# Turning queries and mixed outputs with TensorE's transposition instead of a full product with the mirrored identity

## What is computed

```python
for i in range(DEPTH):                                   # DEPTH = 2
    hn = rmsnorm(h, norm_mix[i])
    if i % 2 == 0:
        h = h + swa_sink_mixer(hn, mem_n, ...)           # 12 heads over a window of 128, 4 memory heads
        h = h + swiglu(rmsnorm(h, norm_ffn[i]), ...)
    else:
        h = h + dilated_mixer(hn, mem_n, ...)            # 3 groups of 4 dilated heads, 4 memory heads
        h = h + moe_swiglu(rmsnorm(h, norm_ffn[i]), ...) # top 2 of 8 experts
return rmsnorm(h, final_norm)

def swa_sink_mixer(h, mem_n, table, w_in, sinks, w_mem_kv, w_out):
    q, k, v, qm = split(einsum('bsd,de->bse', h, w_in))
    o, _ = banded_attention(q, k, v, bias, SWA_WINDOW - 1, sinks)
    om = memory_attention(qm, mem_n, w_mem_kv)
    return einsum('bse,ed->bsd', concatenate([o, om], axis=-1), w_out)
```

## Time and profile before

| what | value |
|---|---|
| median of three runs | 1370.65 us |
| lowest and highest run | 1369.57 and 1371.57 us |
| span of the profiled execution, from its first to its last instruction | 1369.3 us |
| PE busy | 1346.9 us, 98% |
| DVE busy | 1130.6 us, 83% |
| ACT busy | 968.0 us, 71% |
| read from HBM | 431.60 MB, 316 GB/s over the span |

### The profile page before, as it was taken

How to read it: one execution, slowest core, us unless ns; L and a number is a source line. 1 busy time by engine, 2 the same in 40 slices (tenths; PEclk the granted TensorE clock), 3 DMA queues, 4 the chain that set the end, 5 groups by cost and what they waited for, 6 DMA issues and landing times.

```text
span 1369.3 us, 18974 instructions
## 1 busy us (share of the span) xinstructions
PE 1346.9 (98%) x6545; PEld 1077.7 (79%) x6545; DVE 1130.6 (83%) x998; ACT 968.0 (71%) x904; POOL 13.7 (1%) x26
## 2 busy tenths in 40 slices
PE   9999999999999999999999999999999999999997
PEld 7888888888887787777777777778777778777775
DVE  6566554444554779999999999999999999999997
ACT  6553643333363468888888888888888887888886
POOL 1100000000000000000000000000000000000000
PEclk9999999999999999999999999999999999999999
DMA  9812655555451049999999999999999999999993
GB/s 375 312 58 107 228 184 184 184 186 189 147 215 62 18 158 400 423 422 422 422 419 357 421 422 422 421 421 367 395 421 422 422 422 393 386 421 422 422 422 162
DMA packets 61402, 433.28 MB, mean 316 GB/s; under 512 B 7066, under 2 KB 7241, under 8 KB 10032
## 3 DMA queue, kind: packets, MB, share of 16 engines
q1 hardware_dynamic: 59312, 426.80, 77.5%
q0 software_dynamic: 1888, 5.78, 1.3%
q10 hardware_dynamic: 160, 0.14, 0.0%
HBM read 431.60 MB, written 1.09 MB: 316 GB/s over the span
## 4 chain that ended last, share of the span: by engine, by line
PE 91%; DVE 4%; ACT 2%; issue 2%; DMA 1%; ACTq 0%; DVEq 0%; SPq 0%
PE ps L1470 20%; PE ps L1472 19%; PE ps L1471 19%; PE ps L1870 6%; PE ps L1869 6%; PE ps L1885 3%; PE ps L1884 3%; DVE wlo L918 2%; PE ps L1915 2%; PE ps L1803 1%; PE ps L1599 1%; PE ps L1572 1%; PE ps L1477 1%; PE ps L1911 1%; PE ps L1923 1%
## 5 line engine op out<-in xcount | busy, mean ns | idle before, releaser
L918 DVE TENSOR_TENSOR wlo<-raw,whi 128x2048 fp32r<-128x2048 f32 (+1 forms) x403 | 908.8, 2282 | 102.0 <-PE ps L1472 62.9
L548 ACT ACTIVATE whi<-raw 128x2048 fp32r<-128x2048 f32 (+1 forms) x403 | 766.2, 1916 | 125.4 <-PE ps L1472 41.9
L1470 PE MATMUL ps<-whi,xhi 128*128 128x512 f32 (+1 forms) x880 | 346.6, 394 | 5.1 <-DVE wlo L918 2.6
L1471 PE MATMUL ps<-wlo,xhi 128*128 128x512 f32 (+1 forms) x880 | 342.0, 389 | 0.0
L1472 PE MATMUL ps<-whi,xlo 128*128 128x512 f32 (+1 forms) x880 | 342.0, 389 | 0.0
L1470 PEld LDWEIGHTS ps<-whi,xhi 128*128 128x128 f32 x880 | 165.3, 188 | 44.7 <-DVE wlo L918 7.5
L1472 PEld LDWEIGHTS ps<-whi,xlo 128*128 128x128 f32 x880 | 165.2, 188 | 34.3
L1471 PEld LDWEIGHTS ps<-wlo,xhi 128*128 128x128 f32 x880 | 165.3, 188 | 32.4
L1870 PE MATMUL ps<-wlo,xhi 128*64 128x512 f32 x392 | 155.2, 396 | 0.0
L1869 PE MATMUL ps<-whi,xhi 128*128 128x512 f32 x392 | 153.6, 392 | 0.0
L1470 PE MATMUL ps<-whi,thi 128*128 128x512 f32 x320 | 127.1, 397 | 0.2
(11 more groups left out here) (253 smaller groups left out, 1097.5 us busy)
## 6 DMA issues: line engine op xcount, KB each, us to landing
raw<-in_moe_up SPq DMA_DIRECT2D x112, 1024.0 KB, 9.8
raw<-in_moe_gate SPq DMA_DIRECT2D x112, 1024.0 KB, 10.1
raw<-in_moe_down SPq DMA_DIRECT2D x112, 1024.0 KB, 9.7
raw<-in_ffn_up SPq DMA_DIRECT2D x14, 1024.0 KB, 4.8
raw<-in_ffn_gate SPq DMA_DIRECT2D x14, 1024.0 KB, 4.8
raw<-in_ffn_down SPq DMA_DIRECT2D x14, 1024.0 KB, 4.8
raw<-in_dil_w_in SPq DMA_DIRECT2D x10, 1024.0 KB, 4.8
raw<-in_swa_w_in SPq DMA_DIRECT2D x4, 1024.0 KB, 19.5
```

The costliest lines, as they stand in the source:

```text
L548: act.activation(whi[:, c % HIS, 0:span(c)], raw[:, c % RAW, 0:span(c)], ACT.Copy).then_inc(hi_ready, 1)
L918: dve.tensor_tensor(wlo[:, c % LOS, 0:n], raw[:, c % RAW, 0:n], whi[:, c % HIS, 0:n].bitcast(F32), ALU.subtract).then_inc(lo_ready, 1)
L1470: pe.matmul(dst, ahi, bhi, start=start, stop=False)
L1471: pe.matmul(dst, ahi, blo, start=False, stop=False)
```

## The change

Both full products with `anti` become transpositions whose second operand is `anti`. Operands, places in the order, semaphores and everything on the other engines stay as they are: 32 instructions on L1545 and 24 on L1488 are of the other kind afterwards.

```diff
@@ -1484,10 +1484,7 @@
                         kt = 4 * half + j
                         rows_ = memx if op == T_MEM else hn
                         dst, src = ps[:, b, j * P:(j + 1) * P], rows_[:, t, kt * P:(kt + 1) * P]
-                        if turned:
-                            last = pe.matmul(dst, src, anti, start=True, stop=True)
-                        else:
-                            last = pe.transpose(dst, src, ident)
+                        last = pe.transpose(dst, src, anti if turned else ident)
                     last.then_inc(tr_done, 1)
 
             def norm_transposed(k, op, t):
@@ -1542,8 +1539,7 @@
 
 
                         for t in range(TILES):
-                            pe.matmul(ps[:, 0, t * P:(t + 1) * P], proj[:, t, q:q + 2 * HD], anti, start=True,
-                                      stop=True)
+                            pe.transpose(ps[:, 0, t * P:(t + 1) * P], proj[:, t, q:q + 2 * HD], anti)
                         for t in range(TILES):
                             if layer == 0 and n < NH:
 
```

## The result

In the runs with which the change was timed, the kernel takes 1363.72 us (median of five, 1361.82 to 1366.74), before 1370.65 (1369.57 to 1371.58). The ratio is 0.995, with a 95% interval of 0.9935 to 0.9965. The profiled execution of it is the slowest of the five, with a span of 1364.9 us against 1369.3.

The account below looks back on a forecast made before the run. PE was taken to bound attention, with another ring close. Savings of 2.84 + 0.45 + 0.91 + 0 + 0.42 = 4.6 us from the median 1370.65 gave 1366.0 us, range 1364.2 to 1368.3.

Parts of the forecast that it names:

- Attention: Turning the queries by one pass instead of two was to save 1.42 us a layer, 2.84 us for both layers.
- the change of work: In a steady attention pair, some 0.06 us for PE's switch from another kind of work was expected to stay.
- the ring's 3.36: In attention, the loop of scores, DVE, exponential, copy, scores takes 3.36 us, just under PE's forecast period of 3.39 us.
- The first pair: In each layer's attention, PE, ACT's copy and the scores follow with nothing else in the way; 0.22 us saved.
- the last: Eighth pair of attention: its copy stands behind ACT's own work, so the scores can be early by only 0.10 us.
- The outputs: Output products: layer 0 saves 0.45 us at tile 0 and 0.91 at tile 1, layer 1 saves 0 and 0.42.
- tile 0 of layer 1: Output product: DVE begins `xlo` straight after its own `hn`, so earlier transposes are hidden; 0 us saved.
- the unsteady term: At the gather before the experts, PE's clock fall may be met fully, partly or not; about 1.2 us either way.
- the ring caps attention: Rival: the loop through DVE and ACT limits attention's gain to 0.10 us a steady pair; 1367.0 us, chance 0.09.
- the place in layer 0 that I named: Rival: the clock falls once more at the output product, where PE idles until `xlo`; 1367.7 us, chance 0.07.
- The slower rival: One-pass transpositions do not hold PE's clock in attention; 1406 us if both attentions ran low throughout, chance 0.03.

Follow-up runs that it names:

- queries_only: The changed kernel, but the mixed outputs are still turned by the full product, only the queries by transpositions; 1366.51 us, ratio 0.9972.
- twice: The changed kernel with each transposition by the mirrored identity issued two times into the same place, keeping the earlier number of passes; 1369.11 us, ratio 0.9993.
- after_late: The changed kernel with five more warming products ahead of the attention of layer 1; 1367.68 us, ratio 0.9977.
- before_late: The kernel before the change with five more warming products ahead of the attention of layer 1; 1370.77 us, ratio 1.0009.
- again: The changed kernel run once more, unaltered, beside new runs of the kernel before; 1364.90 us, ratio 0.9957.
- again2: The changed kernel run a third time, unaltered; 1363.70 us, ratio 0.9948.
- early: The changed kernel, but PE turns the next pair straight after the scores and ACT copies it ahead of the exponential; 1362.56 us, ratio 0.9944.

## Why the prediction was wrong

**The direction and the mechanism of the saving were right.** A full product of float32 is two passes, a transposition one, at equal price a pass; fewer passes are saved time where PE is the bound. Records, periods and the parts of the output products came as described. The Trainium skill's factor of four for float32 ("TensorE: Matmul & The Clock Gate", Terms) does not hold here: 8 blocks take 0.88 us instead of 1.78.

**The terms, summed to 4.6, are 5.06.** Attention was put at 2.84 us and is 3.22 (queries_only). I let 0.06 us for the change of work stay with the first transposition, so that PE's period would be 3.39; it goes (0.22 us for two turned queries, and 0.45 for four passes in twice), PE alone would come to an estimated 3.61 - 0.28 = 3.33, and the ring's 3.36 took over. That is 0.03 us a pair more. The first pair gave 0.27 instead of 0.22, and the last exactly the 0.10 that were forecast. The outputs were put at 1.78 and gave 1.84: 0.50 for 0.45 and 0.91 in layer 0, nothing at tile 0 of layer 1, where DVE is late, and 0.4 at tile 1. This alone would have put the time at 1370.65 - 5.06 = 1365.6, inside the range.

**The step that failed is the unsteady term.** The prediction said that whether the fall of the clock meets the gather "may differ once all comes 4.6 us earlier: about 1.2 us either way", and so gave it a mean of nothing in the sum, without a reason. It has a sign. The kernel before loses 1.8 us there on average: 1370.4 over all its runs against 1368.6 with the wait filled. The changed kernel loses nothing measurable (0.1 us, -0.7 to 0.9). I had taken the moment of the fall to be spread evenly over executions whatever the kernel. It is not: whether the gather meets a fall hangs on how long after the first rise of the clock its wait comes, and the change moved it by 5 us, from a place that meets falls to one that met none in three traces with the wait unfilled. after_late shows it by moving that place by 1.8 us: the loss is back, and filling the waits takes it away again. before_late points the same way, less clearly. 5.06 us of work and about 1.5 us of this make the 6.5 us between the means of all runs of both kernels (1370.4 and 1363.9).

**How far it was off.** The time lies only 0.5 us below the range, and the median of again, 1364.90, lies inside it; over all 16 runs of the changed kernel the median is 1363.7, outside. The 1.2 us given for this term in either direction was also too little for the 1.8.

**The rivals.** That the ring caps attention came true in its mildest form, 3.36 us. The profiled execution has two falls of the clock in PE's work (layer 1 and the end), where that of the kernel before has one, but not at the place in layer 0 that I named, where PE now idles for 1.13 us; again and again2 have none. The slower rival is not seen: in twice, with 56 full products replaced by 112 transpositions, the clock in attention stays at 1.00. The Trainium skill has the rule behind it ("TensorE: Matmul & The Clock Gate", Part 4: PE-mode transpose): transposes do not count as busy for the clock as products do. No stretch of attention here runs on transpositions alone, so no run shows whether it holds.

**What stays open.** Why some distances from the first rise meet a fall and others do not was not settled, only that they do. The traces at an unfilled gather are eleven, one execution each. How often the kernel before meets a fall was not counted, only what the falls cost on average. In four of the five falls traced there the 32 passes take 1.3 to 1.5 us more than 3.93, in the fifth 2.65, so a mean of 1.8 would need a fall in nearly every execution, or some cost behind the gather too (an estimate from these rows). And the 5.06 us are read up to the gather only. From the gather's end to the span's end the traces differ by more than the kernels do: 863.6 to 867.1 us in the fifteen without a fall in the experts. That the experts themselves gain or lose nothing by the change rests on the medians and means with filled waits, 4.7 us apart (3.9 to 5.4).

## What to carry to other kernels

Turning a float32 tile with a mirrored identity is one pass as a transposition and two as a product, so a float32 tile that is only permuted need not be a full product. Where a kernel has a short wait of TensorE ahead of dense work, an edit far ahead of it can gain or lose nearly 2 us, as here, by moving that wait; fill the wait in both kernels before comparing, or part of the difference may not be the edit's. When one engine's share in a loop is cut, look up the next ring beforehand and also the first and last turn of the loop: here the earlier turning gave 0.02 us a pair in the middle and 0.8 us between the first two.

## What was not expected of the hardware

The price of added work can depend on where it moves a wait: 1.8 us of warming products, placed over 60 us ahead of the gather, cost the changed kernel 3.7 us and the kernel before 0.8 (-0.2 to 2.0). And a transposition after the value product begins without the 0.06 us that a full product lost there, while after the scores it costs 0.27 instead of 0.22 us for two (80.50 to 80.77 in early).
